# Output and gate products of a decoder layer by token halves, norm roots on ten columns

## The chip, the cores and the metric

The kernel runs on one core of one Trainium2 chip. The metric is the device time of one launch in microseconds, from the chip, as a median over runs. The profile comes from one execution of its own.

## What is computed

One layer step for 512 prompt tokens and 8 sample tokens (520 columns in all), model width 1024. The input projection and both attentions come first and are not touched. The change lies in what follows them (names of the reference):

```python
    merged = jax.nn.sigmoid(ga) * u_a + jax.nn.sigmoid(gb) * u_b
    x = x + rmsnorm(merged @ w_out, g_post)
    x = x + jax.nn.sigmoid(x @ w_ple_gate) * rmsnorm(p_i @ w_ple, g_ple)
```

`rmsnorm` divides each token by the root of its mean square over 1024 channels and scales by a vector. `w_out` and `w_ple_gate` are 1024x1024, `w_ple` is 256x1024. The results are both token sets' `x`, and the caches, which are written earlier.

## The kernel before

**Layout.** Activations lie transposed: 128 channels on the partitions, 8 chunks of channels, 520 token columns. A product tile makes 128 output channels for all tokens. fp32 accuracy comes from a split: a weight tile and its activations are each kept as a rounded part (`w_hi`, `h_hi`) and a remainder (`w_lo`, `h_lo`), and each chunk takes three passes, hi*hi, hi*lo and lo*hi. A tile of 8 chunks is 24 passes for each of two column halves of 260.

**Weight ring.** `w_raw`, `w_hi` and `w_lo` have three slots each. SP's queue loads tile n into `w_raw` once the remainder of tile n-3 is made; ACT rounds it (`hi_part`, L1061) once PE is through with the slot; DVE subtracts (`lo_part`, L1315; POOL does it for the `w_ple` tiles, L665).

**The tail.** After eight branch tiles (`TILE_BR`), whose results DVE gates into `gsig` (L1650 to L1653) and ACT and POOL split into `h_hi` and `h_lo` (L1228, L650), come three groups of eight tiles:

- out: `merged @ w_out`. ACT and DVE copy a half each out of PSUM to `yT` (L1236, L1672), ACT squares it (L1241), POOL adds the squares to `acc_y` (L658).
- ple: `p @ w_ple`, two chunks a tile. ACT copies both halves to `eT`. After its second tile a product with a matrix of ones (L1016) spreads the column sums of `acc_y` over all partitions; DVE scales them, ACT takes Ln and Exp for a first inverse root, DVE refines it on 128x520 (`norm`, `rsqrt`). DVE then updates `xT` chunk by chunk (L1687, L1688), ACT rounds the chunk (L1245), POOL makes its remainder (L677).
- gate: `x @ w_ple_gate`, which takes all 8 chunks of the new x. ACT applies the sigmoid (L1292). Ahead of its third tile the same norm is made for `eT` (`acc_e`, L679 and L684). DVE forms the result (`final`: L1696, L1699, L1702), PE turns it back to token rows (`result`, L1035), DVE copies it out (L1604), SP's queue stores it.

Two PSUM banks, `pj0` and `pj1`, serve the halves; a tile's half waits until the same half of the tile before is copied out. Each engine's order is written by hand, and engines wait for counters (semaphores) of one another: an engine that waits holds back all that stands behind it in its program.

## Time and profile before

| | |
|---|---|
| median of 3 runs | 720.85 us (720.31 to 722.61) |
| profiled execution | 720.05 us, its span 718.0 us |
| PE busy | 649.2 us, 90% of the span |
| DVE, ACT, POOL busy | 357.4, 248.6, 175.0 us |
| mean granted TensorE clock | 0.955 of full |

Times in rows count from the span's start. PE is TensorE's matmuls, PEld its weight loads, DVE, ACT and POOL are VectorE, ScalarE and GpSimd, SP is the engine that issues most transfers. A busy share near 90% over the span hides stretches where PE stands; they are looked up by window.

### The profile page before, as it was taken

What the parts mean: (1) busy time and instruction counts of PE and PEld (TensorE: products, weight loads), DVE (VectorE), ACT (ScalarE), POOL (GpSimd) and SP (SyncE); (2) the same over time, 40 slices, a digit from 0 to 9 for tenths busy, and PEclk for the clock granted to TensorE, in tenths of its full rate; (3) what the DMA queues carried; (4) which work ended last, traced back from release to release, by engine and by line L of the source; (5) the groups of instructions that cost most, each with busy time, mean ns of one, the idle gap of its engine ahead of it and who ended that gap; (6) DMA issues with size and microseconds to landing.
All of it is one profiled execution on the core that took longest, in us unless ns stands there. A gap on an engine that the chain in (4) does not pass through costs nothing.

```text
span 718.0 us, 12479 instructions
## 1 busy us (share of the span) xinstructions
PE 649.2 (90%) x4740; PEld 589.1 (82%) x4740; DVE 357.4 (50%) x759; ACT 248.6 (35%) x539; POOL 175.0 (24%) x187
## 2 busy tenths in 40 slices
PE   2989999999999999999898789999999899736992
PEld 2688999899898999999898789565589899736992
DVE  1955455555545444445576664221157531592762
ACT  5553343433434324325121233221113332735310
POOL 3613011010100400002477780101012222465000
PEclk9799999999999999999999999999999999968997
DMA  8069462562521762332499967354524320323111
GB/s 240 20 166 344 150 205 56 182 193 71 183 52 46 237 211 82 89 78 71 122 297 316 320 185 223 105 181 142 163 75 110 89 67 24 90 59 87 44 46 60
DMA packets 105545, 98.42 MB, mean 137 GB/s; under 512 B 6355, under 2 KB 93703, under 8 KB 105200
## 3 DMA queue, kind: packets, MB, share of 16 engines
q1 hardware_dynamic: 101872, 71.64, 34.8%
q0 software_dynamic: 3568, 25.99, 10.1%
q8 instruction: 38, 0.62, 0.4%
q14 instruction: 19, 0.16, 0.1%
q10 hardware_dynamic: 48, 0.01, 0.0%
HBM read 90.31 MB, written 26.14 MB: 162 GB/s over the span
## 4 chain that ended last, share of the span: by engine, by line
PE 70%; DVE 10%; DMA 5%; ACT 3%; issue 3%; SPq 3%; POOL 3%; POOLq 0%; DVEq 0%; ACTq 0%
PE pj L790 47%; PE tr L782 5%; PE pv L740 4%; PE pv L926 3%; PE sc L893 3%; DMA kv_b<-in_cache_b_kv_dram 3%; PE sc L901 2%; PE pv L744 2%; DVE yT L1687 1%; DVE w_lo L1315 1%; POOL prod L623 1%; PE sc L790 1%; PE sc L898 1%; DMA x_in<-in_x_prompt_dram 1%; DVE xT L1688 1%
## 5 line engine op out<-in xcount | busy, mean ns | idle before, releaser
L790 PE MATMUL pj<-h_hi,w_hi 128*128 128x260 f32 x1088 | 323.8, 298 | 31.4 <-DVE w_lo L1315 11.0
L790 PE MATMUL pj<-h_lo,w_hi 128*128 128x260 f32 x1088 | 313.4, 288 | 0.0
L790 PE MATMUL pj<-h_hi,w_lo 128*128 128x260 f32 x1088 | 313.1, 288 | 0.0
L790 PEld LDWEIGHTS pj<-h_hi,w_hi 128*128 128x128 f32 x1088 | 211.3, 194 | 47.1 <-issue 29.3
L790 PEld LDWEIGHTS pj<-h_lo,w_hi 128*128 128x128 f32 x1088 | 211.6, 194 | 0.0
L790 PEld LDWEIGHTS pj<-h_hi,w_lo 128*128 128x128 f32 x1088 | 211.2, 194 | 0.0
L1315 DVE TENSOR_TENSOR w_lo<-w_raw,w_hi 128x1024 fp32r<-128x1024 f32 (+1 forms) x76 | 92.9, 1227 | 59.1 <-ACT w_hi L1061 58.6
L1061 ACT ACTIVATE w_hi<-w_raw 128x1024 fp32r<-128x1024 f32 (+2 forms) x84 | 81.5, 972 | 96.1 <-PE pj L790 40.0
L1322 DVE COPY probT<-tr 128x256 f32<-128x256 f32 (+3 forms) x56 | 27.3, 488 | 52.6 <-PE tr L782 52.6
L623 POOL TENSOR_TENSOR prod<-kv_a,qbc 128x512 f32<-128x512 f32 x24 | 33.8, 1434 | 18.6 <-DMA kv_b<-in_cache_b_kv_dram 13.6
L1413 DVE TENSOR_TENSOR zsil<-zsil,pj 128x260 f32<-128x260 f32 x12 | 4.6, 422 | 50.0 <-ACT zsil L1136 50.0
L926 PE MATMUL pv<-v_tok,probT 128*128 128x64 f32 x216 | 29.4, 263 | 0.0
L740 PE MATMUL pv<-kv_a,pTa 128*64 128x512 f32 x64 | 29.2, 598 | 0.0
L1155 ACT ACTIVATE prob<-sc,nm_a 128x128 f32<-128x128 f32 (+3 forms) x32 | 16.9, 528 | 33.1 <-DVE nm_a L1422 33.1
L926 PEld LDWEIGHTS pv<-v_tok,probT 128*128 128x128 f32 x216 | 27.9, 191 | 0.0
L646 POOL TENSOR_TENSOR og_lo<-og_raw,og_hi 128x512 f32 x6 | 7.6, 1265 | 76.1 <-ACT og_hi L1221 76.1
L1134 ACT ACTIVATE gsig<-pj 128x260 f32<-128x260 f32 x32 | 11.6, 381 | 41.6 <-PE pj L790 41.6
L782 PE MATMUL tr<-const,prob 128*128 128x128 f32 x140 | 25.6, 283 | 0.0
L569 POOL DMA_DIRECT2D out_dram<-k_tok x4 | 3.2, 800 | 89.6 <-DVE k_tok L1322 89.6
L1396 DVE TENSOR_SCALAR samp<-pj 128x8 f32<-128x8 f32 x30 | 4.9, 162 | 38.4 <-PE pj L790 38.4
L893 PE MATMUL sc<-k_aug,q_aug 66*128 66x128 f32 (+3 forms) x64 | 23.4, 454 | 0.0
L1555 DVE TENSOR_REDUCE lg_a<-prod 128x8 f32<-128x512 f32 x24 | 16.4, 685 | 12.7 <-POOL prod L623 12.7
(328 smaller groups left out, 952.5 us busy)
## 6 DMA issues: line engine op xcount, KB each, us to landing
w_raw<-in_w_in_dram SPq DMA_DIRECT2D x52, 512.0 KB, 4.6
kv_a<-in_cache_a_kv_dram SPq DMA_DIRECT2D x64, 256.0 KB, 3.4
out_dram<-in_cache_b_kv_dram POOLq DMA_DIRECT2D x16, 1022.0 KB, 10.1
qbc<-q_dram SPq DMA_DIRECT2D x8, 640.0 KB, 5.7
kv_b<-in_cache_b_kv_dram SPq DMA_DIRECT2D x32, 128.0 KB, 3.1
w_raw<-in_w_out_dram SPq DMA_DIRECT2D x8, 512.0 KB, 4.0
w_raw<-in_w_ple_gate_dram SPq DMA_DIRECT2D x8, 512.0 KB, 4.2
x_in<-in_x_prompt_dram SPq DMA_DIRECT2D x4, 512.0 KB, 6.2
```

The lines of the kernel that those rows point to most:

```text
L623: nc.gpsimd.tensor_tensor(prod[k % PRODS][:, :], kv_a[s][:, i, :], qbc[s][:, 0:AW], ALU.mult).then_inc(S["s_prod"], 1)
L740: nc.tensor.matmul(pv[0][0:DEC * AH, :], pTa[:, p, s, :, :].rearrange("p s h -> p (s h)"), kv_a[s % 2][:, p, :], start=s == 0 and p == 0, ...
L744: last = nc.tensor.matmul(pv[1][0:DEC * BH, 0:BO], pTb[0:n, g, s, :, :].rearrange("p s h -> p (s h)"), kv_b[s % 2][0:n, g, :], start=s == ...
L782: last = nc.tensor.transpose(b[0:rows, c0:c0 + k], src, ident[0:k, 0:k])
L790: ins = nc.tensor.matmul(out, w[:, k0, :], x[:, c_x, lo:hi], start=first and i == 0, stop=last and i == 2)
L893: nc.tensor.matmul(b[:, 0:n], q_aug[s][:, hd, qb * P:n], k_aug[s][:, hd, 0:n], start=True, stop=False)
L926: last = nc.tensor.matmul(pv[u % 2][:, 0:HD], p, v, start=j == 0, stop=j == n - 1)
L1061: nc.scalar.activation(w_hi[n % RING][:, 0:k, :], w_raw[n % RING][:, 0:k, :], ACT.Copy).then_inc(s_hi, 1)
L1155: last = nc.scalar.activation(prob[u % 2][:, 0:n], sc[u % 2][:, 0:n], ACT.Exp, bias=nm_a[:, u % 8:u % 8 + 1], accum_out=l_a[:, u % 8:u % 8 ...
L1315: V.tensor_tensor(w_lo[n % RING][:, 0:k, :], w_raw[n % RING][:, 0:k, :], w_hi[n % RING][:, 0:k, :].bitcast(F32), ALU.subtract).then_inc(s_ ...
L1322: last = V.tensor_copy(dst, src(b))
L1555: V.tensor_reduce(dst, src, AX.X, ALU.add).then_inc(S["s_red"], 1)
```

## The change

The tail is one list of 32 tiles, `TAIL`: four ple tiles, eight out tiles, four ple tiles, eight gate tiles, each run as two jobs, tokens 0 to 255 and 256 to 519. In the out and gate groups the job of a tile's second half comes three tiles after that of its first (`LAG` = 4): h0 of tiles 0 to 3, then h1 of tile 0, h0 of 4, h1 of 1, and so on, with four h1 jobs at the end. Jobs take four PSUM banks in turn, and ACT copies all of them out. `w_hi` and `w_lo` get six slots for the tail; `w_raw` keeps three. The inverse roots are made on token columns (two, three and five of them, each 128 tokens tall) by an integer first guess and three Newton steps on DVE, and PE spreads them. DVE, no longer POOL, makes the `w_ple` weights' remainders, the remainder of x and the sums of `acc_y`; POOL keeps the sums of `acc_e`. Results leave by halves through four buffers.

```diff
+LAG = 4
+WIDE = 2 * RING
...
+            for j in range(len(tiles) + LAG):
+                if j < len(tiles):
+                    seq.append((tiles[j], 0))
+                if j >= LAG - 1 and j - LAG + 1 < len(tiles):
+                    seq.append((tiles[j - LAG + 1], 1))
...
+        def split_before(j):
+            found = []
+            for i in range(RING + 2, len(TAIL)):
+                at = max(FIRST_JOB[i] - 8, LAST_JOB[i - WIDE] + 1 if i >= WIDE else 0)
+                if at == j:
+                    found.append(i)
+            return found
...
             for m in range(DC):
-                hi_part(TILE_BR + m + RING)
+                hi_part(TILE_BR + m + RING if m < 7 else TILE_T + 3)
+                if m >= 6:
+                    hi_part(TILE_T + 2 * m - 10)
...
+            for m in range(1, DC):
+                pool.wait_ge(S["s_sqe"], m + 1)
+                if m > 1:
+                    pool.wait_ge(S["s_ace"], m - 1)
+                nc.gpsimd.tensor_tensor(acc_e[:, :], acc_e[:, :], sq2[m % 2][:, :], ALU.add).then_inc(S["s_ace"], 1)
```

PE (the job itself, and what stands between jobs):

```diff
+            def tail_job(j):
...
+                if half == 0:
+                    wait_parts(pe, n)
+                if j >= 4:
+                    pe.wait_ge(S["s_ev"], j - 3)
...
+                for c in range(kc):
...
+                    if kind == "g" and m == 0:
+                        pe.wait_ge(S[f"s_xl{half}"], c + 1)
+                    ins = product(banks[j % 4][:, 0:hi - lo], slot(n), c, x_hi, x_lo, c, (lo, hi), c == 0, c == kc - 1)
+                ins.then_inc(S["s_job"], 1)
...
+            for j in range(len(JOBS)):
+                tail_job(j)
+                if j == JOB["o", DC - 1, 0] + 1:
+                    pe.wait_ge(S["s_acy"], 2 * DC - 2 - LAG)
+                    mean_square(acc_y, 0, (0, 1))
+                if j == JOB["o", DC - 1, 0] + 2:
+                    pe.wait_ge(S["s_rst"], 1)
+                    spread(0, 0, sc[0]).then_inc(S["s_bct"], 1)
+                if j == JOB["p", 4, 1]:
+                    pe.wait_ge(S["s_acy"], 2 * DC - 2)
+                    mean_square(acc_y, 0, (2, 3, 4))
+                if j == JOB["p", DC - 1, 1]:
+                    pe.wait_ge(S["s_rst"], 2)
+                    spread(0, 1, sc[1]).then_inc(S["s_bct"], 1)
+                if j == JOB_G + 2:
+                    pe.wait_ge(S["s_ace"], DC - 1)
+                    mean_square(acc_e, 5, (0, 1, 2, 3, 4))
+                if j == JOB_G + 3:
+                    pe.wait_ge(S["s_rst"], 3)
+                    spread(5, 0, pv[1])
+                    spread(5, 1, pv[0]).then_inc(S["s_bct"], 1)
+                t = j - JOB_G - 5
+                if 0 <= t < 4:
+                    result(2 * t)
+                    result(2 * t + 1)
+                elif t >= 4:
+                    result(t + 4)
+            result(2 * DC - 1)
```

ACT (in the loop over jobs):

```diff
+                for k in split_before(j):
+                    hi_part(TILE_T + k)
+                act.wait_ge(S["s_job"], j + 1)
...
+                if j == JOB["o", DC - 1, 1] - 1:
+                    x_hi(0, 0, 1)
+                if j == JOB["o", DC - 1, 1]:
+                    x_hi(0, 2, 3)
+                if j == JOB["p", 4, 0]:
+                    x_hi(0, 4, 5)
+                if j == JOB["p", 5, 0]:
+                    x_hi(0, 6, 7)
+                if j == JOB["p", DC - 1, 1]:
+                    x_hi(1, 0)
+                t = j - JOB_G
+                if t == 0:
+                    x_hi(1, 1, 2)
+                    ple_square(4)
+                    ple_square(5)
+                if t == 1:
+                    x_hi(1, 3, 4)
+                    ple_square(6)
+                    ple_square(7)
+                if t == 2:
+                    x_hi(1, 5, 6)
+                if t == 3:
+                    x_hi(1, 7)
```

DVE:

```diff
+            def inverse_root(at, n, turn_):
...
+                link(V.tensor_scalar(v, pv[0][:, 500 + at:500 + at + n], 1.0 / D, EPS, ALU.mult, ALU.add))
+                link(V.tensor_scalar(t.bitcast(I32), v.bitcast(I32), 1, None, ALU.logical_shift_right))
+                link(V.tensor_scalar(y.bitcast(I32), t.bitcast(I32), -1, 0x5F3759DF, ALU.mult, ALU.add))
+                for i in range(3):
+                    link(V.scalar_tensor_tensor(t, v, -0.5, y, ALU.mult, ALU.mult))
+                    link(V.tensor_tensor(t, t, y, ALU.mult))
+                    last = V.scalar_tensor_tensor(y, t, 1.5, y, ALU.add, ALU.mult)
...
+            def x_sum(half, *cs):
...
+                for c in cs:
+                    link(V.tensor_tensor(yT[:, c, lo:hi], yT[:, c, lo:hi], sc[half][:, 0:hi - lo], ALU.mult))
+                    V.tensor_tensor(xT[:, c, lo:hi], xT[:, c, lo:hi], yT[:, c, lo:hi], ALU.add).then_inc(S[f"s_xs{half}"], 1)
+                    if c:
+                        x_lo(half, c - 1)
+                    if c == DC - 1:
+                        x_lo(half, c)
...
+                for k in split_before(j):
+                    lo_part(TILE_T + k)
...
+                if j == JOB["p", 4, 0]:
+                    inverse_root(2, 3, 2)
+                    x_sum(0, 6, 7)
+                if j == JOB["p", 5, 0]:
+                    x_sum(1, 0, 1)
+                if j == JOB["p", 6, 0]:
+                    x_sum(1, 2, 3)
+                if j == JOB["p", 7, 0]:
+                    x_sum(1, 4, 5, 6, 7)
+                t = j - JOB_G
+                if t == 3:
+                    inverse_root(5, 5, 3)
+                    dve.wait_ge(S["s_bct"], 3)
+                if 4 <= t < 8:
+                    final(2 * t - 8)
+                    final(2 * t - 7)
+                if t >= 8:
+                    final(t)
+                if 6 <= t < 10:
+                    result_out(2 * t - 12)
+                    result_out(2 * t - 11)
+                if t >= 10:
+                    result_out(t - 2)
```

**ACT at the start of the tail.** Where before has the first out tile copied and squared between weight roundings (first piece), the change has the first ple jobs (second piece; `tr0` to `pj1` are the four banks in turn, `w_hi2` and `w_hi3` the rounding of out tiles 2 and 3).

```order
L1228 ACTIVATE h_hi_54<-gsig_75 128x520
L1236 ACTIVATE yT_76<-pj0 128x260
L1241 ACTIVATE sq2_0_172<-yT_76 128x520
L1061 ACTIVATE w_hi0_59<-w_raw0_56 128x1024
L1236 ACTIVATE yT_76<-pj0 128x260
```

```order
L1302 ACTIVATE h_hi_54<-gsig_75 128x520
L1328 ACTIVATE eT_77<-tr0 128x256
L1133 ACTIVATE w_hi2_61<-w_raw2_58 128x1024
L1328 ACTIVATE eT_77<-tr1 128x264
L1133 ACTIVATE w_hi3_178<-w_raw0_56 128x1024
L1328 ACTIVATE eT_77<-pj0 128x256
L1133 ACTIVATE w_hi4_180<-w_raw1_57 128x1024
```

In the change three whole weight tiles' roundings (out tiles 1, 2, 3, in `w_hi2`, `w_hi3`, `w_hi4`) stand among the copies of the first jobs; between the last two pieces shown is the copy of `pj1`.

**ACT at the first gate tile.** Before (first piece): the x chunks are rounded, then `eT` is squared, with one sigmoid table load. Now (second piece): the rounding of gate tile 4's weights (`w_hi5`) stands ahead of the last two ple copies, and the squares of `eT` behind the first two sigmoids.

```order
L1061 ACTIVATE w_hi0_59<-w_raw0_56 128x1024
L1245 ACTIVATE h_hi_54<-xT_53 128x520 x4
L1254 ACTIVATE sq2_0_172<-eT_77 128x520
L1254 ACTIVATE sq2_1_173<-eT_77 128x520
L1254 ACTIVATE sq2_0_172<-eT_77 128x520
L1292 ACT_TABLE_LOAD
L1292 ACTIVATE sg0_180<-pj0 128x260
```

```order
L1133 ACTIVATE w_hi5_190<-w_raw2_58 128x1024
L1328 ACTIVATE eT_77<-pj0 128x256
L1328 ACTIVATE eT_77<-pj1 128x264
L1311 ACTIVATE h_hi_54<-xT_53 128x264
L1133 ACTIVATE w_hi0_59<-w_raw0_56 128x1024
L1339 ACTIVATE yT_76<-tr0 128x256
L1311 ACTIVATE h_hi_54<-xT_53 128x264 x2
L1317 ACTIVATE sq2_0_172<-eT_77 128x520
L1317 ACTIVATE sq2_1_173<-eT_77 128x520
L1339 ACTIVATE yT_76<-tr1 128x256
L1311 ACTIVATE h_hi_54<-xT_53 128x264 x2
L1317 ACTIVATE sq2_0_172<-eT_77 128x520
```

There is no table load left in the tail. ACT's squares of the second four ple tiles now stand behind a weight rounding, two copies, a second rounding and a sigmoid.

**DVE while x is updated.** Before (first piece), two instructions a chunk with one weight remainder among them; now (second piece) three a chunk and half, and the remainders of gate tiles 1 and 2 (`w_lo2`, `w_lo3`) behind the twelve small instructions of a root and the last chunks of the first half.

```order
L1687 SCALAR_TENSOR_TENSOR yT_76<-yT_76,g_all_52,rs_y_176 128x520
L1688 TENSOR_TENSOR xT_53<-xT_53,yT_76 128x520
L1315 TENSOR_TENSOR w_lo1_63<-w_raw1_57,w_hi1_60 128x1024
L1687 SCALAR_TENSOR_TENSOR yT_76<-yT_76,g_all_52,rs_y_176 128x520
L1688 TENSOR_TENSOR xT_53<-xT_53,yT_76 128x520
```

```order
L1746 SCALAR_TENSOR_TENSOR rs2_183<-half_v_184,rs2_183 128x3
L1760 TENSOR_TENSOR yT_76<-yT_76,sc0 128x256
L1761 TENSOR_TENSOR xT_53<-xT_53,yT_76 128x256
L1754 TENSOR_TENSOR h_lo_55<-xT_53,h_hi_54 128x256
L1760 TENSOR_TENSOR yT_76<-yT_76,sc0 128x256
L1761 TENSOR_TENSOR xT_53<-xT_53,yT_76 128x256
L1754 TENSOR_TENSOR h_lo_55<-xT_53,h_hi_54 128x256 x2
L1380 TENSOR_TENSOR w_lo2_64<-w_raw2_58,w_hi2_61 128x1024
L1380 TENSOR_TENSOR w_lo3_179<-w_raw0_56,w_hi3_178 128x1024
L1760 TENSOR_TENSOR yT_76<-yT_76,sc1 128x264
```

What POOL did for x (one instruction a chunk) has moved onto DVE, and the factor `gpost` has moved to ACT's copy.

## Rows read from the trace of the kernel before

**Rows 1.** Busy time by windows; after the window its length, then each engine, clock, DMA.
```profile
612.00:630.20 18.20, 13.50 (x100) 12.37 (x98) 10.95 (x13) 14.97 (x31) 9.31 (x9) 1.00 0.38 108
630.20:641.20 11.00, 0.00 (x1) 0.00 (x0) 10.86 (x11) 4.68 (x8) 7.04 (x5) 0.63 0.00 0
641.20:663.70 22.50, 16.97 (x100) 16.22 (x100) 8.86 (x8) 10.03 (x16) 13.05 (x9) 0.80 0.34 95
663.70:703.00 39.30, 39.28 (x315) 38.97 (x316) 24.37 (x34) 10.84 (x18) 0.00 (x0) 0.96 0.16 48
```
**Rows 2.** The timeline of PE: start, length, engine, line, idle time before, its releaser.
```profile
568.22 0.29 PE L790 MATMUL pj<-h_lo,w_hi 128*128 128x260 f32 x1
568.34 0.28 PE L790 MATMUL pj<-h_hi,w_lo 128*128 128x260 f32 x1
...
615.34 1.04 PE L1016 MATMUL pv<-acc_y,const 128*128 128x260 f32 x4
...
641.22 0.59 PE L790 MATMUL pj<-h_hi,w_hi 128*128 128x260 f32 x1 [11.02 <-DVE w_lo L1315]
652.86 0.36 PE L790 MATMUL pj<-h_hi,w_hi 128*128 128x260 f32 x1 [3.04 <-ACT sg L1292]
663.71 0.46 PE L790 MATMUL pj<-h_hi,w_hi 128*128 128x260 f32 x1 [2.48 <-DVE nv L1680]
702.83 0.60 PE L1035 MATMUL sc<-const,fin 128*128 128x128 f32 x4
703.26 0.27 PE L1037 MATMUL pv<-const,fin 128*8 128x128 f32 x1
```
**Rows 3.** The timeline of ACT.
```profile
568.66 0.39 ACT L1236 ACTIVATE yT<-pj 128x260 f32<-128x260 f32 x1 [2.28 <-PE pj L790]
572.07 0.64 ACT L1241 ACTIVATE sq<-yT 128x520 f32<-128x520 f32 x1 [3.02 <-DVE yT L1672]
572.61 1.04 ACT L1061 ACTIVATE w_hi<-w_raw 128x1024 fp32r<-128x1024 f32 x1
574.43 0.39 ACT L1236 ACTIVATE yT<-pj 128x260 f32<-128x260 f32 x1 [0.78 <-PE pj L790]
613.32 0.37 ACT L1259 ACTIVATE eT<-pj 128x260 f32<-128x260 f32 x1
613.58 0.38 ACT L1261 ACTIVATE eT<-pj 128x260 f32<-128x260 f32 x1
```
**Rows 4.** The timeline of DVE.
```profile
16.16 0.17 DVE L1328 TENSOR_TENSOR nt<-nt,nv 128x5 f32<-128x5 f32 x1
16.36 0.17 DVE L1329 TENSOR_SCALAR nt<-nt 128x5 f32<-128x5 f32 x1
...
563.30 0.41 DVE L1650 TENSOR_TENSOR gsig<-gsig,pj 128x260 f32<-128x260 f32 x1
563.64 0.41 DVE L1651 TENSOR_TENSOR gsig<-gsig,sc 128x260 f32<-128x260 f32 x1
565.56 1.22 DVE L1315 TENSOR_TENSOR w_lo<-w_raw,w_hi 128x1024 fp32r<-128x1024 f32 x1
...
631.13 0.70 DVE L1688 TENSOR_TENSOR xT<-xT,yT 128x520 f32<-128x520 f32 x1
633.57 1.66 DVE L1688 TENSOR_TENSOR xT<-xT,yT 128x520 f32<-128x520 f32 x1
...
708.13 0.69 DVE L1604 COPY tok_out<-sc 128x512 f32<-128x512 f32 x1 [1.36 <-DMA out_dram<-tok_out]
```
**Rows 5.** The timeline of POOL.
```profile
584.32 1.31 POOL L658 TENSOR_TENSOR acc_y<-acc_y,sq 128x520 f32<-128x520 f32 x1 [4.35 <-ACT sq L1241]
631.30 3.37 POOL L677 TENSOR_TENSOR h_lo<-xT,h_hi  x2 [1.43 <-ACT h_hi L1245]
```
**Rows 6.** The page's DMA issues (KB, us to landing), and line L396's own view (weight loads).
```profile
w_raw<-in_w_out_dram SPq DMA_DIRECT2D x8, 512.0 KB, 4.0
DMA to landing us min/median/max: 2.1/3.9/5.8
```

More of the change, by code:

```diff
@@ L690, in _ @@
             pool.wait_ge(S["s_sst"], 16 * 8)
-            pool.wait_ge(S["s_yst0"], 16 * DC // 2)
-            pool.wait_ge(S["s_yst1"], 16 * DC // 2)
+            for i in range(4):
+                pool.wait_ge(S[f"s_yst{i}"], 16 * DC // 2)
             pool.wait_ge(S["s_ysst"], 16)
@@ L1011, in _ @@
                     turn([(P, c * DEC, ps_in[:, c * P:(c + 1) * P]) for c in range(2)])
-            def mean_square(total_, ready, done):
-                pe.wait_ge(S[ready], DC)
-                for half, (lo, hi) in enumerate(HALVES):
-                    last = nc.tensor.matmul(pv[half][:, 0:HALF], ones, total_[:, lo:hi], start=True, stop=True)
-                last.then_inc(S[done], 1)
-            for n in range(TILE_OUT, TILE_PLE):
-                for k in range(4):
-                    project(n, k, h_hi, h_lo, "s_ml" if n == TILE_OUT else None)
@@ new lines, in _, with mean_square, spread @@
+            tokens = (0, P, 2 * P, 3 * P, T - P)
+            def mean_square(total_, at, blocks):
+                for b in blocks:
+                    last = nc.tensor.matmul(pv[0][:, 500 + at + b:501 + at + b], total_[:, tokens[b]:tokens[b] + P], ones[:, 0:1], start=True, stop=True)
+                last.then_inc(S["s_msy"], 1)
+            def spread(at, half, out):
+                for b in (0, 1) if half == 0 else (2, 3):
+                    last = nc.tensor.matmul(out[:, b % 2 * P:b % 2 * P + P], rs2[:, at + b:at + b + 1].to_broadcast([P, P]), ident, start=True, stop=True)
+                if half:
+                    last = nc.tensor.matmul(out[:, 2 * P:2 * P + DEC], rs2[:, at + 4:at + 5].to_broadcast([P, P]), ident[:, P - DEC:P], start=True, stop=True)
+                return last
@@ new lines, in result @@
+            def result(r):
+                i, half = JOBS[JOB_G + r]
+                m = TAIL[i][1]
+                pe.wait_ge(S["s_fin"], r + 1)
+                if r >= 2:
+                    pe.wait_ge(S["s_tte"], r - 1)
+                for b in range(2):
+                    last = nc.tensor.transpose(sc[r % 2][:, b * P:(b + 1) * P], xT[:, m, (2 * half + b) * P:(2 * half + b + 1) * P], ident)
+                if half:
+                    last = nc.tensor.transpose(sc[r % 2][0:DEC, 2 * P:3 * P], xT[:, m, SEQ:T], ident)
+                last.then_inc(S["s_tt"], 1)
```

338 lines of the change are left out of this document (150 added, 188 removed).

## The prediction

> **What bounds the kernel now.** I read the windows of the tail first [rows 1]. From 641.2 to 703.0 PE is nearly full; from 630.2 to 641.2 it does nothing while DVE is busy for 10.86 of 11.0 us. So the tail is PE's products plus holes. The timeline of PE names the holes' releasers [rows 2]: 11.02 us ahead of the first gate tile (DVE updating x), 3.04 ahead of its second half, 2.48 at the second norm. The holes cost a second time in the granted clock, whose levels are 2.4 GHz and 1.2 GHz: 0.80 over the 22.5 us behind the first is (1-0.80)x22.5 = 4.5 us of halved clock's loss, 0.96 over the next 39.3 is 1.6 us [rows 1]. In all 16.5 us of holes and 6.1 of clock are what a rearrangement can win. The last product ends at 703.0, the last copy at 708.8 [rows 4], the span at 718.0.
>
> **The part of the sum that stays.** Passes start 0.12 us apart for 260 columns [rows 2]; an out or gate tile is 48 passes, 5.77 us (ACT's copies at 568.66 and 574.43 [rows 3]). Sixteen of them are 92.3 us, eight ple tiles of 12 passes 11.5. Halves of 256 and 264 columns add up to the same 520. The tail's first product can start near 562.9, when the two remainders of p are made: there the change has two small weight remainders for one large.
>
> **Added small products on PE.** A transpose costs 0.11 (four from 702.83 to 703.26 [rows 2]); 37 of the 40 stand before the last product: 4.1 us. The norm's products: 520 columns against a full matrix took 1.04 us [rows 2], so 2.0 us for spreading both norms' columns; the ten one-column sums have no row; between 0.02 (their share of columns) and 0.26 (a full 128 columns) each, I take 0.12: 1.2 us. Together 7.3.
>
> **The start of the tail.** ACT has out tile 2's weight rounding ahead of the copy of the third ple job, tile 3's ahead of the fourth. The load of tile 2 waits for the remainder of the tile three before, a small one behind DVE's last gating (DVE is free at 565.6 [rows 4]), so it is issued near 565.8 and lands 4.0 later [rows 6], 569.8. Rounding 1.05, copy 0.3 [rows 3]: the third copy is done at 571.2, and the seventh job, which needs that bank, starts there, not at 566.4. Out tile 3's load follows the remainder of tile 0 (566.9) and another 512 KB, lands near 571.3; the copies behind its rounding end at 573.0 and 573.4 starts the first out product. Without the wait it were 562.9+8x0.72 = 568.7. **Cost 4.7.** Nothing is behind it: the twelve jobs to the end of out tile 7's first half are 34.6 us, to 608.
>
> **Norm of y and update of x.** The holes of 11 us go, since 11.5 us of second-half jobs and 5.8 of ple jobs lie behind the first half. The root is twelve chained small instructions at 0.20 (16.16 to 16.36 [rows 4]), 2.4 us; against the before's Ln, Exp and 128x520 steps. PE waits 0.5 for it. But DVE now makes three instructions a chunk and half: 0.46 (0.43 and the link), 0.33, 0.33 (pitch of 563.30 to 563.64 [rows 4]), 1.12 us, 8 chunks 9.0 a half. It can go past the first two chunks only at 618.8, since ACT's rounding of chunk 0 stands behind the copy of job o6h1. From there: 7 chunks 7.3, the remainders of gate tile 0, 1, 2 (1.14 each) 3.4, the second root 2.4, two small ones 0.7: gate tile 1's remainder ends at 632.2. ACT stands for DVE's chunks 6 and 7 ahead of the ple copies, PE wants their banks. The last out product ends at 621.2, the first gate product starts at 632.8; its own work there is 6.8 (8x0.72, sums 0.4, spread 0.6). **Cost 4.8, with the 0.5: 5.3**, against 11.0 before.
>
> **The second norm.** This is the term on which the sign hangs. Gate tile 4's load waits for the remainder of tile 1, 632.2, lands 636.2 [rows 6]. Its rounding stands on ACT ahead of the last two ple copies, and these ahead of everything in the order shown: roundings 1.05x2, copies 0.54, a chunk 0.3, to 639.3; sigmoid and two chunks 0.8; squares of tiles 4 and 5, 1.1; sigmoid and two chunks, the second waiting for DVE's chunk 4 (x of the second half is late by the same stop), to 645.1; squares 6 and 7 to 646.3; POOL's four additions of 1.31 [rows 5] end at 648.4. PE is through with gate tile 2 at 641 and waits there for the seventh addition: 7.7 us. DVE and POOL also meet. An addition on DVE took 0.70 alone and 1.66 while POOL worked, and POOL's pair 3.37 for 2x1.31 [rows 4, 5]; with four POOL additions between DVE's, the hole is 9.4. **Cost 8.5**, between the two, since part of DVE's instructions there read PSUM. The Trainium skill (SBUF, Who interferes with whom) says that a DVE instruction with two SBUF inputs and a GpSimd one that reads SBUF exclude each other for the whole instruction; the trace agrees in that 1.66. By that rule the hole is the 9.4 and the forecast 0.9 longer; by the page's other case, one input from PSUM, the multiplications of x_sum are free of it.
>
> **The third root.** PE next runs gate tile 3's first half and then waits for the root of ten columns' last five. Ahead of it on DVE stands the remainder of chunk 7, whose rounding on ACT stands behind that very job's sigmoid: 0.4+0.4+0.4, a weight remainder 1.1, root 2.4. **Cost 4.8**, once.
>
> **Results.** In four places PE takes two results after a job, and the copy that frees their bank stands on DVE behind the result of that same job: sigmoid 0.4, two steps of 0.43, copy 0.4, hand-overs. **Cost 4x1.9 = 7.7**. Before had no such wait, since results ran two whole tiles behind their product. The first of the four is not of this kind: there DVE is behind by what the third root cost.
>
> **Clock.** The 2.48 hole was followed by 1.6 us of loss, the 3.04 by about 1.7 and the 11.0 by 2.8 (4.5 together [rows 1]). Two holes of such size stay, so 3.3 to 5.6; none if the fall misses them. I take 3.4. **Hand-overs** (0.02 in my steps, up to 0.2 at POOL in the trace) are some ten more: 1.0.
>
> **Sum.** 562.9 + 103.8 + 7.3 + 4.7 + 5.3 + 8.5 + 4.8 + 7.7 + 3.4 + 1.0 = 709.4 for the last product, 703.0 before. Behind it: sigmoid, two half steps, two or three transposes, a copy, 2.7 us where before took 5.8 (it waited for a store of its two buffers; now four). Last copy 712.1, then the same 9.2 of store and end: span 721.3. The profiled execution stood 2.05 over its span: **723.4**, I say 723.5; the median before is 0.8 over that execution's 720.05, so this is 2.7 over the median. The table loads that go hide behind the second ple tiles and the second norm: I give them nothing beyond the holes counted.
>
> **Rivals.**
> - **A, faster, 713.5.** Weights come in time: if the remainder of gate tile 1 is done by about 628 instead of 632.2, the fourth tile's load has landed when ACT gets to it, the squares run 4 us earlier, the chunks of the second half follow (4 us for the load and some 3 for what ACT and DVE then no longer hold up for one another), so the 8.5 becomes 1.5, and one fall of the clock goes (1.7), and one of the four waits at the results, where DVE is behind (1.2): 723.4-7-1.7-1.2 = 713.5. For it: ACT was busy 4.68 of 11.0 us before [rows 1], it has room. Against: the 13 us of DVE work above stand in series.
> - **B, no change, 719.** The order is as forecast, but DVE and POOL hardly meet (-0.8) and the clock holds over both holes (-3.4). For: PE was busy for only 13.50 of the 18.20 us from 612.0 and the clock stayed at 1.00 [rows 1]. Against: the three others did not.
> - **C, much slower, 729.** Loads of 5.8 us [rows 6] instead of 4.0, at the start and at gate tile 4: +3.6, and the clock at its upper price, +2.2.
> - **D, the trailing does not do its work.** If the first gate half had to wait for the x of all tokens, the start at 632.8 would move behind the second half's chunks, nine us on; the jobs' waits (each half has counters of its own) all but exclude it, and what chance it has is in C's.
>
> **How the numbers follow.** The forecast has 0.31, A 0.27, B 0.27, C and D 0.15. What this measurement can tell from no change is about 0.3%, 2.2 us: 718.7 to 723.0. A is faster (0.27); B, and nothing else wholly, is the same (0.27); forecast and C are slower (0.46). The range takes A with 1.5 us below it and C with 2 above: 712 to 731; the forecast's own, by the bounds of its terms (clock 1.6 to 5.6, the hole 7.7 to 9.4, ten sums 0.2 to 2.6), is 720 to 727.
>
> **What would show it.** After the change PE's timeline should have: first out product near 573; gate products from near 633 (before 641); a hole of 7 to 10 us released by POOL's `acc_e` after the third gate job; one of near 5 released by DVE's `rs2`; short ones released by `tok_out`. No hole at `acc_e` makes the forecast wrong on A's side; a first gate product after 637 on C's.

## The result

| | kernel before | changed kernel |
|---|---|---|
| median | 720.91 us (720.31 to 722.61, 4 runs) | 734.46 us (731.74 to 742.12, 4 runs) |
| ratio to before | | 1.0201 (95% interval 1.0122 to 1.028) |
| profiled execution, its span | 720.05, 718.0 us | 735.5, 733.3 us |
| mean granted clock | 0.955 | 0.943 |
| PE, DVE, ACT, POOL busy | 649.2, 357.4, 248.6, 175.0 us | 661.9, 366.5, 241.5, 147.6 us |

The change makes the kernel 2.0% slower, 13.6 us. The forecast was 723.5, so its sign holds and its size does not: the time lies outside the range of 712 to 731.

### The profile page after: what moved, and what is told of

Read it like the earlier page. It is cut to its first block, busy times and chain, and to the rows that moved or that the text cites. A ratio compares the mean times of both kernels' runs of the same rounds, so it can differ in the third digit from the quotient of the medians.

```text
span 733.3 us, 12572 instructions
## 1 busy us (share of the span) xinstructions
PE 661.9 (90%) x4772; PEld 601.1 (82%) x4772; DVE 366.5 (50%) x868; ACT 241.5 (33%) x552; POOL 147.6 (20%) x164
## 4 chain that ended last, share of the span: by engine, by line
PE 70%; DVE 11%; DMA 6%; POOL 3%; issue 3%; ACT 3%; SPq 2%; POOLq 0%; DVEq 0%; ACTq 0%
PE pj L813 40%; PE tr L813 5%; PE tr L805 5%; PE pv L763 4%; PE pv L949 3%; PE sc L916 3%; PE sc L924 2%; DVE w_lo L1380 2%; PE pv L767 2%; DMA kv_b<-in_cache_b_kv_dram 2%; POOL prod L674 2%; POOL prod L678 1%; DMA qbc<-q_dram 1%; PE sc L813 1%; DMA x_in<-in_x_prompt_dram 1%
## 5 line engine op out<-in xcount | busy, mean ns | idle before, releaser
L813 PE MATMUL pj<-h_hi,w_hi 128*128 128x260 f32 (+2 forms) x960 | 286.6, 298 | 13.2 <-ACT gsig L1206 10.4
L813 PE MATMUL pj<-h_lo,w_hi 128*128 128x260 f32 (+2 forms) x960 | 276.4, 288 | 0.0
L813 PE MATMUL pj<-h_hi,w_lo 128*128 128x260 f32 (+2 forms) x960 | 276.0, 288 | 0.0
L813 PEld LDWEIGHTS pj<-h_hi,w_hi 128*128 128x128 f32 x960 | 186.7, 194 | 27.7 <-issue 25.1
L1380 DVE TENSOR_TENSOR w_lo<-w_raw,w_hi 128x1024 fp32r<-128x1024 f32 (+2 forms) x84 | 95.5, 1141 | 45.1 <-ACT w_hi L1133 44.5
L813 PE MATMUL tr<-h_hi,w_hi 128*128 128x264 f32 (+1 forms) x128 | 39.2, 306 | 0.0
L813 PE MATMUL tr<-h_lo,w_hi 128*128 128x264 f32 (+1 forms) x128 | 38.1, 298 | 0.0
L813 PE MATMUL tr<-h_hi,w_lo 128*128 128x264 f32 (+1 forms) x128 | 38.0, 297 | 0.0
L674 POOL TENSOR_TENSOR prod<-kv_a,qbc 128x512 f32<-128x512 f32 x24 | 34.4, 1460 | 17.1 <-DMA kv_b<-in_cache_b_kv_dram 12.1
L763 PE MATMUL pv<-kv_a,pTa 128*64 128x512 f32 x64 | 29.2, 599 | 0.0
L813 PEld LDWEIGHTS tr<-h_lo,w_hi 128*128 128x128 f32 x128 | 26.6, 208 | 0.0
L813 PEld LDWEIGHTS tr<-h_hi,w_hi 128*128 128x128 f32 x128 | 26.5, 207 | 0.0
L813 PEld LDWEIGHTS tr<-h_hi,w_lo 128*128 128x128 f32 x128 | 26.2, 205 | 0.0
L805 PE MATMUL tr<-const,prob 128*128 128x128 f32 x140 | 25.7, 283 | 0.0
## 6 DMA issues: line engine op xcount, KB each, us to landing
out_dram<-in_cache_b_kv_dram POOLq DMA_DIRECT2D x16, 1022.0 KB, 10.2
```

Of the source, the lines that this page charges most:

```text
L674: nc.gpsimd.tensor_tensor(prod[k % PRODS][:, :], kv_a[s][:, i, :], qbc[s][:, 0:AW], ALU.mult).then_inc(S["s_prod"], 1)
L763: nc.tensor.matmul(pv[0][0:DEC * AH, :], pTa[:, p, s, :, :].rearrange("p s h -> p (s h)"), kv_a[s % 2][:, p, :], start=s == 0 and p == 0, ...
L805: last = nc.tensor.transpose(b[0:rows, c0:c0 + k], src, ident[0:k, 0:k])
L813: ins = nc.tensor.matmul(out, w[:, k0, :], x[:, c_x, lo:hi], start=first and i == 0, stop=last and i == 2)
L1380: V.tensor_tensor(w_lo[slot(n)][:, 0:k, :], w_raw[n % RING][:, 0:k, :], w_hi[slot(n)][:, 0:k, :].bitcast(F32), ALU.subtract).then_inc(s_lo, 1)
```

## The profile after

**PE's holes.** The timeline of PE answers to [rows 2]: start, length, engine, line, idle time before, its releaser.

```profile
574.42 0.36 PE L813 MATMUL pj<-pT_hi,w_hi 128*128 128x256 f32 x1 [2.49 <-ACT eT L1328]
...
576.75 0.41 PE L813 MATMUL tr<-h_hi,w_hi 128*128 128x256 f32 x1
...
635.19 0.39 PE L813 MATMUL pj<-pT_hi,w_hi 128*128 128x264 f32 x1 [2.44 <-ACT eT L1328]
...
636.84 0.56 PE L813 MATMUL tr<-h_hi,w_hi 128*128 128x256 f32 x1
...
654.49 2.29 PE L1064 MATMUL pv<-const,acc_e 128*128 128x1 f32 x10 [7.60 <-POOL acc_e L707]
665.99 2.08 PE L1070 MATMUL pv<-const,rs 128*128 128x128 f32 x8 [4.66 <-DVE rs L1746]
680.74 1.09 PE L1082 MATMUL sc<-const,xT 128*128 128x128 f32 x4 [2.18 <-DVE tok_out L1785]
...
721.15 0.28 PE L813 MATMUL pj<-h_hi,w_lo 128*128 128x264 f32 x1
...
723.77 0.27 PE L1084 MATMUL sc<-const,xT 128*8 128x128 f32 x1
```

The same kernel's waits of PE between 563 and 727 us (summed, how often, the longest), and then before's:

```profile
PE sc L1082 <- DVE tok_out L1785: 10.0, 5, 2.2
PE pv L1064 <- POOL acc_e L707: 7.6, 1, 7.6
PE pj L813 <- ACT eT L1328: 5.2, 3, 2.5
PE pv L1070 <- DVE rs L1746: 4.7, 1, 4.7
```

```profile
PE pj L790 <- DVE w_lo L1315: 11.0, 1, 11.0
PE pj L790 <- ACT eT L1259: 4.7, 4, 2.7
PE pj L790 <- ACT sg L1292: 3.0, 1, 3.0
```

Every hole of the forecast is there, with its releaser and nearly its size: 7.60 us on POOL's sums, 4.66 on the third root, and ahead of the results four of 2.18, 1.89, 2.10 and 2.07 (the fifth of the 10.0 us is at the very end). The big hole of before is gone. With the smaller rows, the tail's holes add up to 29.2 us against 25.1: 4.1 more.

**The clock.** These are windows of the changed kernel, cut at the seven stretches of the tail in which the trace grants half the clock (1.2 GHz); the columns are those of [rows 1].

```profile
574.90:578.30 3.40, 3.40 (x18) 3.40 (x18) 1.59 (x2) 2.68 (x5) 0.00 (x0) 0.50 0.77 212
636.30:639.70 3.40, 3.40 (x18) 3.40 (x18) 2.83 (x6) 0.34 (x2) 0.00 (x0) 0.51 0.54 156
650.00:660.20 10.20, 5.71 (x26) 5.72 (x27) 5.77 (x11) 2.48 (x6) 2.94 (x3) 0.50 0.18 51
663.60:670.40 6.80, 4.42 (x20) 4.42 (x21) 3.93 (x18) 0.00 (x0) 0.00 (x0) 0.50 0.01 2
680.70:684.10 3.40, 3.36 (x16) 3.35 (x17) 3.02 (x6) 0.00 (x0) 0.00 (x0) 0.51 0.28 77
694.40:697.80 3.40, 3.40 (x18) 3.40 (x17) 0.00 (x0) 0.00 (x0) 0.00 (x0) 0.50 0.24 63
701.20:704.60 3.40, 3.40 (x17) 3.40 (x17) 0.00 (x0) 0.00 (x0) 0.00 (x0) 0.50 0.27 77
```

And the same for the kernel before, which had three:

```profile
633.20:646.90 13.70, 5.68 (x25) 5.58 (x26) 13.56 (x11) 3.35 (x5) 8.69 (x6) 0.50 0.20 52
653.70:657.10 3.40, 3.40 (x18) 3.40 (x17) 1.23 (x1) 1.92 (x4) 2.41 (x2) 0.51 0.18 43
663.90:667.30 3.40, 3.40 (x17) 3.40 (x17) 0.95 (x2) 2.35 (x3) 0.00 (x0) 0.50 0.54 154
```

Half the clock costs only where PE works: I reckon the loss at half of PE's busy time in such a stretch. Before that is (5.68+3.40+3.40)/2 = 6.2 us, after it is 27.09/2 = 13.5 us. So the clock takes 7.3 us more than before, which is more than the holes take. Before lost most of its slow time inside one hole of 11 us, where it costs nothing; the change has many small holes, and the slow stretches behind the short ones are full of products.

**DVE in the result stage,** from its timeline. The step L1774 at 686.29 (the sigmoid times the scaled `eT`) waits 2.50 us for the sigmoid of the job that PE has just done; the copies that free `sc` stand behind it, and PE's transposes at 687.65 wait for them.

```profile
683.31 0.48 DVE L1772 SCALAR_TENSOR_TENSOR eT<-eT,g_all,pv 128x256 f32<-128x256 f32 x1
686.29 0.42 DVE L1774 TENSOR_TENSOR eT<-eT,yT 128x256 f32<-128x256 f32 x1 [2.50 <-ACT yT L1339]
686.74 0.42 DVE L1775 TENSOR_TENSOR xT<-xT,eT 128x256 f32<-128x256 f32 x1
687.09 0.74 DVE L1785 COPY tok_out<-sc 128x256 f32<-128x256 f32 x2
```

**POOL and DVE ahead of the second norm** (answers to [rows 4, 5]; POOL's timeline, then DVE's):

```profile
646.28 3.79 POOL L707 TENSOR_TENSOR acc_e<-acc_e,sq 128x520 f32<-128x520 f32 x2 [54.63 <-ACT sq L1317]
651.43 3.00 POOL L707 TENSOR_TENSOR acc_e<-acc_e,sq 128x520 f32<-128x520 f32 x2 [1.35 <-ACT sq L1317]
```

```profile
646.63 2.31 DVE L1380 TENSOR_TENSOR w_lo<-w_raw,w_hi 128x1024 fp32r<-128x1024 f32 x1
649.31 1.06 DVE L1761 TENSOR_TENSOR xT<-xT,yT 128x264 f32<-128x264 f32 x1
...
653.22 1.50 DVE L1754 TENSOR_TENSOR h_lo<-xT,h_hi 128x264 fp32r<-128x264 f32 x1
```

With POOL idle the same instructions take 0.43 us (the sum L1761), 0.42 (the remainder L1754) and 1.22 (the weight remainder L1380). The step L1760, whose second input comes from PSUM, stays at 0.42 throughout.

What starts the sums late is the order on ACT, as forecast: it stands for 4.24 us for the load of gate tile 4's weights, and the last ple copies, the rounding of x and the squares are behind it (ACT's timeline).

```profile
640.89 1.06 ACT L1133 ACTIVATE w_hi<-w_raw 128x1024 fp32r<-128x1024 f32 x1 [4.24 <-DMA w_raw<-in_w_ple_gate_dram]
```

**The part ahead of the tail** is the same code in both kernels, and does not take the same time in each execution. DVE's last gating starts at 568.07 here, at 565.22 before, and between 564.65 and 573.21 in the runs below (DVE's timeline, changed kernel; then the kernel before, with PE's last transpose):

```profile
568.07 0.43 DVE L1718 TENSOR_TENSOR gsig<-gsig 128x260 f32<-128x260 f32 x1
```

```profile
565.22 0.43 DVE L1653 TENSOR_TENSOR gsig<-gsig 128x260 f32<-128x260 f32 x1
...
706.20 0.27 PE L1037 MATMUL pv<-const,fin 128*8 128x128 f32 x1
```

So I compare tails from here on: from the start of that gating to PE's last transpose. That is 141.0 us before (565.22 to 706.20) and 155.7 us after (568.07 to 723.77). It is one execution each; the medians beside it are of several. The two executions of the changed kernel differ by 0.6 us in it.

## The experiments

My theory: the loss lies in places of instructions on ScalarE and VectorE, which make PE stop, and in the granted clock that follows the stops. The rivals: too much work for VectorE, too small products (halves of 256 and 264 columns), the trailing itself, or an accident of the execution.

| kernel | median us | ratio to before (95%) | tail us | half clock in the tail us |
|---|---|---|---|---|
| a, control | 737.51 | 1.0198 (1.0151 to 1.0246) | 156.3 | 34.1 |
| b, copies first | 723.51 | 1.0012 (0.9988 to 1.0035) | 142.4 | 23.9 |
| c, filled holes | 728.43 | 1.0077 (1.0053 to 1.0101) | 148.7 | 10.2 |
| d, late splits and early squares | 728.66 | 1.0097 (1.0069 to 1.0126) | 149.7 | 30.7 |
| e, head's splits late | 732.65 | 1.0136 (1.0097 to 1.0176) | 152.3 | 34.1 |
| f, late splits alone | 734.15 | 1.014 (1.0095 to 1.0185) | 152.8 | 30.7 |
| g, early squares alone | 732.88 | 1.0148 (1.0108 to 1.0188) | 152.2 | 30.7 |
| h, all moves | 708.94 | 0.9817 (0.9783 to 0.985) | 128.7 | 6.8 |
| i, h with root and spread moved | 705.25 | 0.976 (0.9717 to 0.9803) | 123.4 | 6.8 |
| k, filled ahead of results only | 730.82 | 1.0117 (1.0062 to 1.0171) | 151.5 | 23.9 |
| l, trailing by four tiles | 737.1 | 1.021 (1.0154 to 1.0265) | 158.8 | 41.0 |
| n, all moves but the copies | 721.3 | 0.9991 (0.9965 to 1.0016) | 141.6 | 17.1 |

The kernel before stood at 722.22 beside a to d, 722.15 beside e to h, 721.48 beside i to n. The intervals of the ratios of e, f, g and k overlap the control's, and i's that of h: for these the medians by themselves part nothing, and what is said of them rests on the tail of one execution each and on the waits and the clock in it.

The last column is time, not loss. PE's busy time in the slow stretches, halved, is 13.6 us in a, 8.4 in b, 5.2 in c, 13.5 in d, 14.4 in e, 13.8 in f, 12.3 in g, 2.3 in h, 3.1 in i, 8.1 in k, 16.6 in l and 7.5 in n; it was 13.5 in the changed kernel and 6.2 before.

### a. The control

> The changed kernel again, as the control of the runs beside it. Theory: the change costs 10 to 14 us by its own (head 8, holes of engine order and the granted clock after them), so 731 to 735 us against 721 of the kernel before, with the granted clock between the first out product and the last gate product at half speed for 24 to 34 us of stretches, against 20.5 before. Rival (an accident of the execution: the part ahead of the tail, which the change does not touch, came 2.9 us later in the profiled run, and the runs spread from 731.7 to 742.1): then this one comes out within 3 us of the kernel before, and where it does not, its last branch product ends after 565 us by as much as it is slower.

737.51, 15.3 us over before. Its last gating starts at 569.21, 4.0 us later than in before's profile, and its tail is 15.3 us longer. The median lies above the 731 to 735 that I expected. An accident it is not: the tail is long again, with nearly the same holes (29.7 us instead of 29.2) and the same 34.1 us of half clock.

### b. The copies first

```diff
+                if 6 <= t < 10:
+                    result_out(2 * t - 12)
+                    result_out(2 * t - 11)
+                if t >= 10:
+                    result_out(t - 2)
                 if 4 <= t < 8:
                     final(2 * t - 8)
                     final(2 * t - 7)
                 if t >= 8:
                     final(t)
-                if 6 <= t < 10:
...
```

> VectorE's copies out of the results' transposes are put ahead of the final steps of the same turn, so that tok_out comes free before PE asks for it. Theory (the four holes of 2.18, 1.89, 2.10 and 2.07 us in front of the transposes are the order of two things on VectorE, and each is followed by a stretch at half clock): the holes go, the clock stays full from 680 to 725 us, and the time falls by 8 us for the holes and up to 6 for the clock: 721 to 727. Rival 1 (VectorE has too much work in that stage, whatever its order): the holes move to the wait on final (s_fin) and 2 us at most are gained: 731 to 735. Rival 2 (only the holes count, the clock does not follow them): 8 us, 725 to 727, with the half stretches at 680.7, 694.4 and 701.2 still there.

723.51, 14 us less than the control and no different from before. The waits of PE in it, and its windows of the result stage:

```profile
PE pv L1064 <- POOL acc_e L707: 7.7, 1, 7.7
...
PE pv L1070 <- DVE rs L1746: 4.7, 1, 4.7
PE sc L1082 <- DVE xT L1775: 1.2, 1, 1.2
PE sc L1082 <- DVE tok_out L1785: 0.7, 1, 0.7
```

```profile
668.00:680.00 12.00, 12.00 (x99) 11.84 (x98) 9.00 (x20) 3.06 (x5) 0.00 (x0) 0.97 0.08 22
680.00:706.00 26.00, 25.27 (x213) 24.99 (x213) 16.99 (x47) 3.10 (x8) 0.00 (x0) 1.00 0.20 57
```

The waits on `tok_out` fall from 10.0 to 0.7, those at the norms stay, and the clock is full from 680 on. Rival 1 falls: VectorE does the same instructions, was busy for 17 of 26 us, and is in time. Rival 2 falls too: the tail shrinks by 13.3 to 13.9 us, more than the holes (9.3 less on `tok_out`, 1.2 more on `xT`).

### c and k. Products of no use in the holes

```diff
+            def fill(j, n):
+                pe.wait_ge(S["s_ev"], j - 2)
+                for _ in range(n):
+                    nc.tensor.matmul(banks[(j + 1) % 4][:, 0:2 * P], pT_hi[:, 0, 0:P], pT_hi[:, 0, 0:2 * P], start=True, stop=True)
...
+                if JOB_G + 6 <= j <= JOB_G + 9:
+                    fill(j, 12)
                 if j == JOB_G + 2:
+                    fill(j, 45)
...
                 if j == JOB_G + 3:
+                    fill(j, 30)
```

In k the two last additions are left out, so that only the result stage is filled.

> Products of no use (two operands already in the store, a bank that the next job overwrites) are put into PE's queue ahead of the waits on acc_e (45), on the third root (30) and on the results (4 times 12), so that PE computes through the holes; no wait is taken away. Theory (some 13 us of the tail are half clock that the holes bring): the clock stays full from 650 on and the time falls by 5 to 9 us, 726 to 730, though PE does 141 products more. Rival (the clock's falls are not the holes' doing, or the waits set the time anyway): the falls stay where they were, and the time is the same or up to 10 us longer by the added products, 734 to 744.

> The changed kernel with products of no use ahead of the results alone (4 times 12, some 1.4 us each), none in the norm of e. It parts the 13.6 us that the copies first gave into holes and clock. Theory (8.2 us holes, the rest clock): the four holes on tok_out stay as PE's stops of 0.5 to 1 us behind the filler, the stretches at 680.7, 694.4 and 701.2 are at full clock, and the tail is 3 to 5 us shorter than 156.0, so 732 to 734 beside 737.5 of the control. Rival (the clock's falls in the result stage follow from the long holes at 650 to 668): the stretches stay half and nothing is gained.

The rival of each falls: both are faster than the control, by 9.1 and 6.7 us of the medians, though PE does 123 and 48 products more: 7.0 to 7.6 and 4.2 to 4.8 us of the tail. (The expectation's 141 was a miscount. k was measured beside a kernel before that was 0.7 us faster than the control's.) No wait was taken away and no other engine's work was touched, so what is won is the clock's. The loss reckoned from the slow stretches falls by 8.3 us in c and by 5.4 in k, which fits. In c one short stretch was left at the norm (658.7 to 662.1), where I had expected none. The window of k that answers to b's second:

```profile
680.00:706.00 26.00, 23.68 (x195) 22.84 (x196) 13.02 (x34) 1.94 (x5) 0.00 (x0) 1.00 0.17 47
```

The changed kernel had 19.20 us of busy time at a mean clock of 0.80 in this window. With PE's stops there down to 0.45 to 0.76 us the clock holds. So of the 13.6 us that b wins, some 5 are the clock's (4.2 to 4.8 by k; half of the 10.2 us of half clock that b has less than the control, by the table), and the holes are the rest.

### d, f, g. The second norm

```diff
-                at = max(FIRST_JOB[i] - 8, ...
+                at = max(FIRST_JOB[i] - 4 if i >= 20 else FIRST_JOB[i] - 8, ...
...
                 if j == JOB["p", DC - 1, 1]:
+                    for q in range(4, DC):
+                        ple_square(q)
                     x_hi(1, 0)
                 t = j - JOB_G
                 if t == 0:
                     x_hi(1, 1, 2)
-                    ple_square(4)
-                    ple_square(5)
...
```

f has the first edit alone, g the second, d both.

> Two moves of places on ScalarE and VectorE: the splits of gate tiles 4 to 7 four jobs later, and ScalarE's squares of ple tiles 4 to 7 ahead of its rounding of x, so that the sums of POOL and VectorE for the norm of e begin some 10 us earlier. Theory (the hole of 7.60 us in front of the five one-column sums, with the half clock that follows from 650.0 to 660.2 us and the 4.66 us of the third root, is owed to engines that start late): the hole shrinks from 7.6 to under 2 us and the clock with it: 6 to 9 us less, 725 to 729. Rival (the hole is the sums themselves, slowed by POOL and VectorE at one port at the same time: 1.06 to 1.50 us for a sum that takes 0.43 alone): 1 to 3 us less, and the hole stays above 4 us.

> Only the splits of gate tiles 4 to 7 move four jobs later; the squares stay. Theory: with both moves PE's tail was 149.7 us long instead of 155.7 and 156.3 (from the last gating of the branches to PE's last transpose). The splits take 2.31 us each on ScalarE and VectorE, so alone they bring 2 to 3 us of it: 734 to 736 beside 737.5. Rival (the squares alone do it): no change, 737 to 738.

> Only ScalarE's squares of ple tiles 4 to 7 move ahead of its rounding of the second half of x; the splits stay. Theory: POOL's sums begin some 10 us earlier and the hole on acc_e (7.60 us in the changed kernel) falls to 2 or 3, but the last sum lies with VectorE behind x, so 3 to 4 us less: 733 to 735 beside 737.5. Rival (ScalarE's rounding of x, now 4 squares later, holds VectorE's lo parts and PE's gate products of the second half): a new wait of PE on s_xl1 in front of gate job 1 of 2 us or more, and no change or up to 3 us more, 737 to 741.

The hole on `acc_e` is 7.6 us in the changed kernel, 3.4 in f, 2.1 in g and gone in d. POOL's four sums in d, from its timeline:

```profile
634.71 5.67 POOL L707 TENSOR_TENSOR acc_e<-acc_e,sq 128x520 f32<-128x520 f32 x4 [46.16 <-ACT sq L1317]
```

They begin 70.1 us behind the last gating instead of 78.2, and take 1.42 each instead of 1.70. So the hole was in the main a late start, and only 1.1 us of it POOL's slower sums. But PE comes to the next wait earlier, and that on `rs` grows from 4.7 to 5.8 in f, 7.3 in g and 6.2 in d: between a fifth and a half of what was won is given back. The tail is 3 to 4 us shorter by each, 6.0 to 6.6 by both.

What d wins is holes alone: they add up to 23.1 us instead of 29.2, while the loss by the clock is 13.5 us as before. The half of the theory that had the slow stretch of the norm go with its hole did not come true: d has 10.2 us at half clock from 650.3 to 660.5, around the wait on `rs`.

### e. The head of the tail

```diff
+                at = max(i if i < 10 else FIRST_JOB[i] - 8, ...
```

> The splits of the tail's tiles 5 to 9 are moved back by up to four jobs on ScalarE and VectorE (one a job, from job 5 to job 9), so that the first copies of ple banks are not queued behind them. Theory (the stop of PE at job 7, 2.49 us after the copy of eT, and the half clock from 574.9 to 578.3 us are owed to a split that waits for its load in front of the copies): both go, 2 to 4 us less, 731 to 735 beside 737.5 of the control. Rival (the banks wait for PE's own products, or the split's load comes late whatever its place): a stop of 2 us or more stays at another job, and the time is within 1.5 us of the control.

732.65: 4.9 us under the control, 3.4 to 4.0 of it in the tail. The head's window in e, and in the changed kernel:

```profile
572.00:582.00 10.00, 10.00 (x87) 10.00 (x86) 4.90 (x4) 7.14 (x12) 0.26 (x1) 1.00 0.78 227
```

```profile
572.00:582.00 10.00, 7.58 (x51) 7.61 (x52) 4.72 (x5) 6.61 (x13) 0.00 (x0) 0.83 0.80 227
```

The loads take the same share (0.78 and 0.80); only their splits no longer stand ahead of the copies. The slow stretch at the head is gone, but that ahead of the gate tiles is 6.8 us long instead of 3.4 (630.7 to 637.6), so the sum in the table stays at 34.1: what e wins is holes (25.7 us instead of 29.2 and 29.7), not clock.

### l. Does the trailing cost?

```diff
-LAG = 4
+LAG = 5
```

> The second token half trails by four tiles instead of three (one constant), nothing else of the changed kernel's is moved. Theory (the trailing itself costs nothing, PE's stops are the places of the other engines' steps; a wider trail gives the second half of x and the norm of e one job, some 3 us, more): the hole on acc_e is the same or 3 us less, the holes on tok_out stay: 733 to 738. Rival (the trailing is the cost, since leading tiles need their weights sooner, one load and two splits a job instead of one in two): PE stops for w_hi or w_lo by 2 us or more at the first gate jobs, and the time is 739 to 745.

737.1, the control's time, and no wait on `w_hi` or `w_lo`: a wider trail is neither the cure nor the cause. A new hole of 3.5 us on `acc_y` stands for what it might have won, and the hole on `acc_e` grows to 8.8. A narrower trail (LAG 3) was not tried.

### h, n. Do the gains add?

h has the edits of b, d and e, and `x_hi(1, 7)` one job earlier; n is h without that of b.

> The moves together: copies ahead of final steps, the late splits at the gate and at the head, the early squares, and the rounding of x's chunk 7 one job earlier. Nothing is taken out of the kernel. Theory (each hole is an order of engines, the clock follows the holes): the 13.6 us that the copies first gave (tail 142.4 us instead of 156.0), 6.3 of splits and squares (149.7), 3 of the head, 1 to 3 of chunk 7 and the clock that is left: a tail of 130 to 135 us instead of 156, 710 to 716, so 6 to 12 us under the kernel before. Rival (each hole that is taken away only moves the wait to the norm of e or to the loads of the gate's weights, which come at 5 us a tile): 718 to 723, no better than the copies first alone.

> All moves except the first: the copies out of the results' transposes stay behind the final steps. It asks if the gains add. The copies first took 13.6 us of the tail alone (142.4 of 156.0). Theory (the result stage's loss is its own): the tail here is 128.7 + 13 = 142 us, 722 beside 708.9 with the copies first. Rival (with the stages ahead in time, VectorE has caught up and the order in the result stage decides less): 5 us or less, a tail of 130 to 134, 711 to 714.

708.94, better than the 710 to 716 expected, and 721.3. The copies take 12.9 us off the tail in this company (141.6 to 128.7) and 13.3 to 13.9 alone: the result stage's loss is its own. The other moves together take 14.1 us off the changed kernel's 155.7 (n), where d and e by themselves took 6.0 and 3.4. The 4 to 5 us beyond their sum are the clock's: neither d nor e lowered the loss by it, and n has 7.5 us of it instead of 13.5. (n and h also have `x_hi(1, 7)` one job earlier, which no run parts from the rest.)

h is 1.8% faster than the kernel before, without an instruction of the change left out; so the small products are not what makes the change slow, nor is VectorE's work. What is left in it is one long wait on the third root with one slow stretch there, and a wait of 2.44 us on `eT`; first PE's waits, then its busy time and clock by windows:

```profile
PE pv L1070 <- DVE rs L1742: 7.3, 1, 7.3
```

```profile
560.00:640.00 80.00, 75.38 (x619) 74.00 (x619) 48.60 (x103) 40.18 (x88) 12.60 (x9) 1.00 0.35 101
640.00:668.00 28.00, 19.98 (x149) 19.53 (x148) 21.67 (x56) 7.47 (x16) 0.00 (x0) 0.88 0.16 47
668.00:694.70 26.70, 25.54 (x215) 24.99 (x213) 16.37 (x46) 3.12 (x8) 0.00 (x0) 1.00 0.20 56
```

### i. The last long wait

```diff
-                if j == JOB_G + 3:
+                if j == JOB_G + 4:
                     pe.wait_ge(S["s_rst"], 3)
...
-                if t == 3:
+                if t == 2:
                     inverse_root(5, 5, 3)
+                if t == 3:
                     dve.wait_ge(S["s_bct"], 3)
```

> All moves, and two more at the one long wait that is left (7.3 us of PE on rs, 6.8 us at half clock from 647.9): VectorE does the third root ahead of two splits (2.35 us) instead of behind them, and PE spreads it one job later, behind the first gate job of the second half. Theory (that wait too is an order, and the clock follows it): 2.3 us earlier on VectorE and 3 us of products in between, so 2 us of wait or less are left, the half stretch goes, and the time falls by 5 to 8 us under that of all moves: 701 to 704 (708.9 before). Rival (the final steps of VectorE, now begun later, bound the rest): the wait moves to the results' transposes, 707 to 710.

705.25, 2.4% under before, and 5.3 us off the tail of h. The wait on the root is 0.63 us:

```profile
654.02 1.16 PE L1070 MATMUL pv<-const,rs 128*128 128x128 f32 x8 [0.63 <-DVE rs L1742]
```

The median is 3.7 us under h's, where I had expected 5 to 8, and above the 701 to 704 that I gave; the intervals of the two overlap (beside each, the kernel before stood at 722.15 and 721.48). The slow stretch did not go as expected: there is one from 633.0 to 639.8, ahead of this place, at the last wait on `eT`. So i has no less half clock than h; what it wins is the wait.

## Why the prediction was wrong

The forecast had PE's last product at 709.4; it ended at 721.4. In order of time:

- **Start, not forecast: +2.85.** The part ahead of the tail was later by that in this execution. It need not be the change's: the control's was 4.0 later with the same code, d's 0.6 earlier. Of the 13 profiles with the change 12 start later than the one of before, by 3.1 us in the mean of all; but that one is a single execution, and the medians show no such delay: their differences from the kernel before are on average 0.8 us smaller than those of the tails. A forecast for one execution has this uncertainty, and I had given it none.
- **The start of the tail, cost 4.7: right.** First out product forecast at 573.4, measured 576.75, less 2.85 is 573.9; the slow stretch from 574.9, for which the forecast had nothing here, accounts for 0.9 of it. e showed its cause as named: splits ahead of copies. (The two roundings that the text ahead of the prediction names first, `w_hi2` and `w_hi3`, are those of out tiles 1 and 2.)
- **Norm of y and update of x, cost 5.3: nearly.** First gate product forecast at 632.8, measured 636.84, less 2.85 is 634.0; so 0.7 more than the start had left. The rest of the slow stretch, 576.75 to 578.3, is 0.8.
- **The second norm, cost 8.5: near in size, 7.60,** and right in what releases it. The size is in part luck: PE came to the wait at 646.9, which less 2.85 is 3.0 us later than the forecast's 641, and the last sum ended some 3 us later than its 648.4, too. The forecast's own terms also give 632.6, not 632.2, for gate tile 1's remainder, and 7.4, not 7.7, between 641 and 648.4. That it hangs on a late start of the squares, d, f and g showed. The ten one-column sums took 2.29 us at half clock; in h, at full clock, 1.17, which is my 1.2.
- **The third root, 4.8: measured 4.66. Results, 7.7: measured 8.2.** b showed the cause of the latter as the text had it, a copy that stands behind the result of the same job.
- **Clock, 3.4 (bounds 1.6 to 5.6): this is the step that failed. It measured 13.5.** From the first gate product to the end of the last product the forecast had 76.6 us and the run 84.6, 8.0 more, while the holes in it were 0.5 smaller than forecast. From 636.84 on PE was busy at half clock for 23.1 us, which is 11.6 us of loss against the 3.4. That makes up 7.7 of the 8.0. Over the whole tail the clock is 10.1 us more than the 3.4; with the 2.85 of the start it more than covers the 12.0 by which the last product was late.

The mistake in that step was in the main one of counting: "two holes of such size stay". I priced a fall of the clock from before's holes of 2.48, 3.04 and 11.0 us, correctly at some 1.7 for a short one, and then charged it only to the two holes of the norm. The four I had myself forecast ahead of the results (1.9 each, in fact 2.06 on average; three of them brought a slow stretch), and the wait in the head (2.49 in fact), are of the size of the 2.48 that before had shown to cost it; charged to each of them, the term would have been five falls more, 8.5 us, and the sum near 732. Part is size: the two holes of the norm alone brought 17.0 us of slow stretches with 10.1 us of PE's busy time in them, a loss of 5.1 where the forecast had 3.4. (The fifth short stretch of the run was not behind one of the four, but behind the last wait on `eT`.)

The rivals: A needed the hole on `acc_e` to close, B the clock to hold; neither did. C had a price near the result (729), but by slow loads. The out tiles' did land later (the page's DMA issues of the changed kernel; 4.0 in [rows 6]), but the first out product was only 0.5 us later than forecast, and the clock is enough to account for that:

```profile
w_raw<-in_w_out_dram SPq DMA_DIRECT2D x8, 512.0 KB, 4.8
w_raw<-in_w_ple_gate_dram SPq DMA_DIRECT2D x8, 512.0 KB, 4.1
```

C's other half, the clock at its upper price of 5.6, was less than half of what it took. D did not come either: the first gate half began within 1.2 us of the forecast's time, once the start is taken off, and at 636.84 it lies just inside the 637 that the forecast set as C's sign. What stands between the tails of before and after, 14.7 us, is 7.3 of clock, 4.1 of holes, and 3.3 that I did not part further, PE's own small products among them.

## What to carry to other kernels

Count the stops of PE, and do not go by their sum alone: one hole of 11 us cost 2.8 us of clock here, and holes of 2 us cost up to 1.7 each, nearly their own length again. But do not expect the clock to come back with each hole that goes: d and e took away holes of 7.6 and 2.5 us and won no clock, while the moves together did. When work is cut into halves, look on the evacuating engine for a copy that frees a bank behind a step that waits for the job just done; putting the copy ahead took no instruction away and gave 14 us. And measure a move against an interval of the program that starts behind the part that did not change.
